# Squares of two input norms summed on GpSimd, TensorE totals four tiles in place of sixteen

## What is computed

```python
def rmsnorm(x, g):
    y = x * lax.rsqrt(jnp.mean(x * x, axis=-1, keepdims=True) + EPS)
    return y * g

# first block, after the mixer
x = x + rmsnorm(mix, post_mix_norm)
hf = rmsnorm(x, pre_ffn_norm)                                # norm "ffn"
ff = (silu(hf @ w_gate) * (hf @ w_up)) @ w_down
x = x + rmsnorm(ff, post_ffn_norm)
# second block
z = rmsnorm(x, norm1_g)                                      # norm "n1"
proj = z @ w_in
...                                                          # pooling mixer, recurrent mixer
h = x + y @ w_out
h = h + peer_ffn(rmsnorm(h, norm2_g))                        # norm "n2"; experts gathered by row
out = rmsnorm(h, norm_f_g)
```

## Time and profile before

| | us |
|---|---|
| median of 3 runs (lowest to highest) | 2685.85 (2684.73 to 2687.1) |
| the profiled execution | 2679.96 |
| its span, first to last instruction | 2678.1 |
| TensorE busy in the span | 2266.4 |
| VectorE busy | 2128.2 |
| ScalarE busy | 1023.7 |
| GpSimd busy | 701.0 |

### The profile page before, as it was taken

How to read it: one execution, slowest core, us unless ns; L and a number is a source line. 1 busy time by engine, 2 the same in 40 slices (tenths; PEclk the granted TensorE clock), 3 DMA queues, 4 the chain that set the end, 5 groups by cost and what they waited for, 6 DMA issues and landing times.

```text
span 2678.1 us, 32043 instructions
## 1 busy us (share of the span) xinstructions
PE 2266.4 (85%) x11484; PEld 1811.8 (68%) x11484; DVE 2128.2 (79%) x3112; ACT 1023.7 (38%) x1509; POOL 701.0 (26%) x834
## 2 busy tenths in 40 slices
PE   8999989999999999989899964444555558999997
PEld 7997778888888888879888831111222225777776
DVE  6986647665566566577766999999999999999997
ACT  5433554443444344454542011000234324544443
POOL 1000000000000000000002353433434442889884
PEclk9999999999999999999999976665676669999999
DMA  6533445555555555544558999999999996999996
GB/s 226 188 122 107 125 143 173 188 188 188 183 187 186 189 181 180 175 133 154 189 176 360 422 419 420 419 420 419 417 403 390 409 402 216 367 403 409 395 396 250
DMA packets 314374, 730.97 MB, mean 273 GB/s; under 512 B 21025, under 2 KB 223009, under 8 KB 275745
## 3 DMA queue, kind: packets, MB, share of 16 engines
q0 software_dynamic: 73728, 402.69, 37.2%
q1 hardware_dynamic: 240402, 325.99, 35.9%
q10 hardware_dynamic: 144, 1.05, 0.1%
HBM read 727.57 MB, written 2.10 MB: 272 GB/s over the span
## 4 chain that ended last, share of the span: by engine, by line
DVE 27%; PE 16%; DMA 10%; issue 4%; POOL 2%; ACT 1%; DVEq 0%; PEldq 0%; ACTq 0%; POOLq 0%
DVE row L2503 13%; DMA row<-in_peer_u,expert 5%; DVE pl L2519 4%; DMA row<-in_peer_v_rows,expert 4%; PE pl L865 4%; PE pl L872 3%; PE pg L1294 3%; DVE hot_b L2544 1%; POOL row L801 1%; PE pl L1259 1%; PE pl L868 1%; PE pl L869 1%; PE pg L1285 1%; PE pl L1188 1%; DMA v_tile<-in_peer_v_dense 1%
## 5 line engine op out<-in xcount | busy, mean ns | idle before, releaser
L1956 DVE TENSOR_TENSOR wlo<-raw,whi 128x1024 fp32r<-128x1024 f32 (+1 forms) x436 | 517.9, 1208 | 373.7 <-ACT whi L1351 372.1
L1351 ACT ACTIVATE whi<-raw 128x1024 fp32r<-128x1024 f32 (+1 forms) x436 | 445.0, 1040 | 410.4 <-PE pl L872 405.9
L2503 DVE CUSTOM_DVE_ANT_0 row<-row,pg 128x2048 f32<-128x2048 f32 x256 | 573.8, 2285 | 25.5 <-DMA row<-in_peer_u,expert 22.2
L1259 PE MATMUL pl<-row,diag 128*128 128x512 f32 x404 | 320.4, 939 | 306.1 <-DMA row<-in_peer_v_rows,expert 260.4
L865 PE MATMUL pl<-x_split,whi 128*128 128x512 f32 x1888 | 478.5, 395 | 9.6 <-DVE x_split L1964 4.6
L1259 PEld LDWEIGHTS pl<-row,diag 128*128 128x128 f32 x404 | 102.4, 279 | 475.6 <-issue 395.8
L865 PEld LDWEIGHTS pl<-x_split,whi 128*128 128x128 f32 x1888 | 341.4, 190 | 73.9 <-issue 7.5
L872 PE MATMUL pl<-x_split,wlo 128*128 128x256 f32 x2656 | 373.1, 283 | 3.9 <-DVE wlo L1956 3.9
L872 PEld LDWEIGHTS pl<-x_split,wlo 128*128 128x128 f32 x2656 | 358.4, 192 | 23.1 <-DVE wlo L1956 4.5
L801 POOL DMA_INDIRECT row<-in_peer_v_rows,expert x256 | 304.9, 1191 | 164.4 <-DVE dots L2503 69.1
L801 POOL DMA_INDIRECT row<-in_peer_u,expert x256 | 241.8, 944 | 372.3 <-DVE dots L2503 168.2
(11 more groups left out here) (347 smaller groups left out, 2941.0 us busy)
## 6 DMA issues: line engine op xcount, KB each, us to landing
v_tile<-in_peer_v_dense SPq DMA_DIRECT2D x128, 512.0 KB
raw<-in_w_in SPq DMA_DIRECT2D x51, 1024.0 KB
raw<-in_w_gate SPq DMA_DIRECT2D x44, 1024.0 KB
raw<-in_w_up SPq DMA_DIRECT2D x44, 1024.0 KB
raw<-in_w_out SPq DMA_DIRECT2D x32, 1024.0 KB
raw<-in_w_down SPq DMA_DIRECT2D x32, 1024.0 KB
wq<-in_peer_wq SPq DMA_DIRECT2D x15, 1024.0 KB, 11.8
raw<-in_w_down SPq DMA_DIRECT2D x16, 768.0 KB
```

Of the source, the lines that this page charges most:

```text
L1259: last = mm(pl_all[:, c:c + width], diag[:, (at - 1) % 4, :], row[b][:, c - DENSE:c - DENSE + width], start=at == 1, stop=at == ADDED_ROWS ...
L1351: return nc.scalar.activation(o, i, ACT.Copy)
L1956: V.tensor_tensor(wlo[:, n % 4, 0:k, :], w[:, :, f, :], whi[:, n % 4, 0:k, :].bitcast(F32), ALU.subtract)\
L2503: V.tensor_tensor_reduce(row[b][:], row[b][:], z_tok[:], 1.0, 0.0, ALU.mult, ALU.add, dots[:, at:at + 1])\
```

## The change

The norms "ffn" and "n1" join the tuple of norms whose squares GpSimd adds; it reads them from `tmp`. `two_groups` no longer has any matmul of squares between its products; behind pieces 4 and 5 stands `wide_total` with four matmuls. The function `squares` goes.

```diff
-ADDED = ("post", "postf", "n2")
+ADDED = ("post", "ffn", "postf", "n1", "n2")
...
             for m, name in enumerate(ADDED):
-                sq = {"post": mix, "postf": mix}.get(name)
+                sq = {"post": mix, "ffn": tmp, "postf": mix, "n1": tmp}.get(name)
                 n = sq_count(NI[name], -1)
...
-                last = sq_r[:, 1] if name == "n2" else mix[:, 14:16, :]
+                last = sq_r[:, 1] if name == "n2" else (tmp if name in ("ffn", "n1") else mix)[:, 14:16, :]
                 pe.wait_ge(norm_sq, sq_count(n, 7))
...
-            def squares(name, g):
-
-                n = NI[name]
-                if g == 0:
-                    pe.wait_ge(norm_inv, n)
-                pe.wait_ge(norm_sq, sq_count(n, g))
-                mm(pnorm, ones[:], tmp[:, 2 * g, :], start=(g == 0), stop=False)
-                last = mm(pnorm, ones[:], tmp[:, 2 * g + 1, :], start=False, stop=(g == 7))
-                if g == 7:
-                    last.then_inc(norm_sum, 1)
...
-                    if x % 2:
-                        squares(name, x // 2)
                 last.then_inc(hi_used, 1)
...
                 half_group(piece + 4, 1, PAIRS[0], arriving=arriving, step_of=2, apart=apart)
-                for g in range(4, 8):
-                    squares(name, g)
+                wide_total(name)
                 half_group(piece + 6, 1, PAIRS[1], apart=apart)
```

## The result

The changed kernel took 2696.84 us as the median of five runs (2693.46 to 2699.60), the kernel before 2685.05 us beside it: a ratio of 1.0045 with an interval of 1.0034 to 1.0056, so 12 us slower. The forecast was 2697.3 us, with a range from 2688 to 2704. The profiled execution took 2693.46 us (its span 2691.6), 13.5 us above that of before.

A forecast was written before the change was run, and what follows sets the result against it. VectorE was taken to bound each norm stage up to the last x_split piece, TensorE after it. Per norm + 5.4 (adds) + 2.0 (clock) - 1.7 (matmuls) = + 5.7 us; 2685.85 + 11.4 = 2697.3 us, range 2688 to 2704.

The forecast's parts named there:

- Who leads: Both norm stages: VectorE bounds up to the last x_split piece, TensorE after it; the first eight matmuls' removal is worth 0.
- What an add costs VectorE: Both norm stages: each GpSimd add ahead of the last x_split piece delays VectorE 1.08 us, 5.4 us per norm.
- How many adds stand ahead: Both norm stages: five adds come before the last x_split piece, the sixth behind it.
- The sixth add: Behind the last x_split piece: it delays three wlo subtractions by 1.1 us, within TensorE's 3.4 us, so costs 0.
- TensorE's clock: Both norm stages: thin work before the last x_split piece halves the clock for 4.0 us, costing 2.0 us per norm.
- The upper bound of half for 6.8 us: Clock term in both norm stages: at most, half clock for 6.8 us, costing 3.4 us.
- Rival 1: Both norm stages: VectorE slowed as forecast but TensorE keeps its clock; + 7.4 us, 2693.2 us; chance 0.24.
- Matmuls saved: Total of each norm: eight matmuls on the path become four, 1.7 us earlier per norm.
- Adds bunched behind the subtractions (2): Both norm stages: GpSimd yields to busy VectorE, adds gather until it is idle; 2700 us; chance 0.08.
- The sixth ahead of the last piece (3): Both norm stages: sixth add also precedes the last subtraction, clock low for 6.8 us; + 16.4, 2702 us; chance 0.07.
- The adds cost nothing (4): Both norm stages: adds cost VectorE almost nothing, leaving 1.7 us gained per norm; 2682.4 us; chance 0.16 with small mixed cases.
- The sum: Both norms together: + 5.7 us per norm, + 11.4 us for both, giving 2697.3 us.

The follow-up runs named there:

- the memsets: The changed kernel with a GpSimd memset in place of each add in the two norms, their sums left out: 2683.77 us (0.9994).
- the fillers: The changed kernel plus unused matmuls of ones and squares behind the first four pairs' products and ahead of the last three x_split waits: 2693.88 us (1.0029).
- the memsets and fillers: The changed kernel with memsets for the two norms' adds and the first eight filling matmuls behind the first products: 2682.78 us (0.9987).
- forced: The changed kernel with all six adds of both norms held back until VectorE has cut the last x_split piece: 2701.83 us (1.0066).

## Why the prediction was right, step by step

- **Who leads.** VectorE up to the last x_split piece, TensorE behind it: held. Every us that VectorE lost appears in the last piece, and the first eight matmuls were fully hidden: with memsets for the adds and the clock held, the second block's total came after 29.12 us without them as with them.
- **What an add costs VectorE.** 1.08 us forecast from the earlier trace rows, 1.03 to 1.08 measured, 5.27 us per norm for 5.4. By the memsets it is the reads. Five adds of 1.30 us in full would have been 6.5 us: VectorE loses the add's 1.30 us less some 0.2, as in the earlier trace rows. The full blocking of the Trainium skill, on the page named above, agrees in kind and not in the whole price.
- **How many adds stand ahead.** Five, by the trace. The second and fourth lose one turn each (2.37 and 2.29 us), which costs VectorE no more than the others.
- **The sixth add.** Expected to end 5.4 us behind 418.3, that is at 423.7 (423.1 in the trace after, which is 0.6 us ahead here), and ended at 426.51; it delayed no wlo subtraction in the FFN's stage. In the second block it did, by 1.1 us, as forecast. Cost 0 in both, but in the FFN's stage by a margin of 1.35 us and not 3.4: there this step was right in its result and wrong in its reason, and with TensorE at full clock both margins were gone.
- **TensorE's clock.** 2.0 us forecast from the earlier trace rows and the first matmuls of the stage, 1.55 and 1.90 us measured, and given back by the fillers (1.1 and 1.6; the rest of each is what the sixth add then costs). The upper bound of half for 6.8 us came from no row; the most that a stage lost, over all these kernels, was 2.5 us, that is half for 5. I had named two reasons for the thin work as one; the experiments show that the slower pieces do it alone, and that the missing matmuls can. Rival 1, the clock holds, fell; its 2693.2 us is near what the filled kernel took, 2693.88.
- **Matmuls saved.** 1.7 us per norm, measured by themselves with the memsets and fillers.
- **Rivals 2 to 4.** Adds bunched behind the subtractions (2): refuted for five of six; forced, they gave 2701.83 us. The sixth ahead of the last piece (3): no. The adds cost nothing (4): no, but its price was right: without the reads and with the clock held, 2682.78 us against 2682.4.
- **The sum.** 11.4 us forecast, 11.8 by the medians, 13.5 in the profiled execution: 10.5 in the stages where 11.4 were expected, and 1.6 at a clock fall in the down projection and some 1.4 between there and 1451, which no step of the prediction had (-0.6 ahead of the first stage and 0.7 behind 1451 make up the rest). That the sum fell so near to the median is in part luck, for the place of such falls differs from run to run.

## What to carry to other kernels

An engine that is idle isn't free. Before work goes to GpSimd, look at what VectorE does beside it: an add that reads SBUF stood a VectorE instruction with two SBUF operands still for 1.05 us, to save TensorE two matmuls of 0.43, and of the twelve saved per norm eight had been hidden. Price moved work on both sides: only the part that stood on the path is gained, and what it blocks on the engine that leads is paid. And where TensorE's work gets thin next to a part that leads, look at the granted clock; to make the work on the path cheaper where it stands (here 0.43 to 0.12 us per matmul, at the price of rounded squares) was worth more than to move it.

## What the runs showed of the hardware

- More work on TensorE made it faster: with matmuls used for nothing, the granted clock stayed at 1.00 where it had been 0.50, and the total came 1.1 to 1.6 us earlier.
- At the same place, a wait of 2.0 us left the clock at 1.00 in one profiled execution (before) and was followed by matmuls at half speed in another (after), 1.55 us lost.
- A GpSimd add that began first still lost to three VectorE subtractions in a row (4.78 to 4.80 us for 1.30), in the profile of each of the five kernels that have it there. The Trainium skill, on the page and in the section named above, has it that issue order decides who blocks; the five adds before it fit that, this row doesn't.
- A GpSimd add that depends on the one before starts 0.32 to 0.67 us after its end, where nothing else holds it (the kernel with the adds held back).
